# Half sums of weight blocks: added by GpSimd instead of by accumulating DMAs

## The reference, cut to what matters

```python
D_MODEL = 2048
SEQ = 256
DEPTH = 2
D_FF = 4 * D_MODEL

def sq_relu_mlp(xn, w_up, w_down):
    return jnp.square(jax.nn.relu(xn @ w_up)) @ w_down

def reference(x, ...):
    h = x
    for l in range(DEPTH):
        j = l // 2
        hn = rms_norm(h, mix_norm_g[l])
        if l % 2 == 0:
            h = h + diff_hgrn_mixer(...)
        else:
            h = h + short_conv_mixer(...)
        hn = rms_norm(h, mlp_norm_g[l])
        h = h + sq_relu_mlp(hn, mlp_w_up[l], mlp_w_down[l])
    return rms_norm(h, final_norm_g)
```

## Time and profile before

| | |
|---|---|
| median of 3 runs | 2291.91 us (2291.8 to 2291.96) |
| the profiled execution | 2291.84 us, its span 2289.8 us |
| PE busy | 2256.8 us, 99% |
| DVE busy | 1759.3 us, 77% |
| ACT busy | 1291.2 us, 56% |
| POOL busy | 289.8 us, 13% |
| granted TensorE clock, mean | 0.998 |
| bytes moved | 470.49 MB, 205 GB/s mean |
| the accumulating DMAs | 44.04 MB, 10.3% of the time of the 16 DMA engines |

### The profile page before, as it was taken

One profiled execution on the slowest core, in us unless ns is written; L12 is line 12 of the kernel. 1 busy time (PEld: TensorE's weight loads), 2 busy tenths in 40 slices (PEclk: granted clock), 3 DMA queues, 4 the chain that ended last, 5 costly groups with the idle time before them and its releaser, 6 DMA issues.

```text
span 2289.8 us, 31124 instructions
## 1 busy us (share of the span) xinstructions
PE 2256.8 (99%) x11429; PEld 1902.5 (83%) x11429; DVE 1759.3 (77%) x1882; ACT 1291.2 (56%) x1655; POOL 289.8 (13%) x409
## 2 busy tenths in 40 slices
PE   8999999999999999999999999999999999999997
PEld 7888888878788888888889999998788888888886
DVE  5778788866888888888875564657888888888885
ACT  5555555537666566566555333435665665665663
POOL 4444555510000000000000000000000000000000
PEclk9999999999999999999999999999999999999999
DMA  9555555556778678678656555556687787787754
GB/s 261 166 158 153 159 153 147 167 168 217 210 239 275 193 238 276 197 232 280 182 167 208 180 176 195 190 183 221 182 279 202 224 285 201 223 278 209 219 172 154
DMA packets 324321, 470.49 MB, mean 205 GB/s; under 512 B 13257, under 2 KB 144626, under 8 KB 318706
## 3 DMA queue, kind: packets, MB, share of 16 engines
q1 hardware_dynamic: 318114, 424.92, 56.8%
q0 software_dynamic: 6048, 44.04, 10.3%
q10 hardware_dynamic: 48, 0.02, 0.0%
HBM read 422.79 MB, written 2.10 MB: 186 GB/s over the span
## 4 chain that ended last, share of the span: by engine, by line
PE 90%; DVE 7%; ACT 1%; issue 1%; SPq 1%; DMA 0%; DVEq 0%; POOL 0%; POOLq 0%; ACTq 0%
PE pair L433 18%; PE pair L437 18%; PE pair L435 17%; PE m L1083 7%; PE m L1088 7%; PE m L1086 7%; PE pair L456 3%; PE pair L460 3%; PE pair L458 3%; DVE raw L1781 2%; DVE w_lo L524 2%; PE m L460 1%; PE m L458 1%; PE m L456 1%; PE m L934 1%
## 5 line engine op out<-in xcount | busy, mean ns | idle before, releaser
L520 ACT ACTIVATE w_hi<-raw 128x1024 fp32r<-128x1024 f32 x648 | 663.3, 1056 | 494.5 <-DVE raw L1781 242.9
L524 DVE TENSOR_TENSOR w_lo<-raw,w_hi 128x1024 fp32r<-128x1024 f32 x648 | 764.2, 1221 | 204.5 <-ACT w_hi L520 202.5
L412 DVE TENSOR_TENSOR w_lo<-raw,w_hi 128x1024 fp32r<-128x1024 f32 x320 | 400.1, 1267 | 273.5 <-ACT w_hi L401 272.2
L401 ACT ACTIVATE w_hi<-raw 128x1024 fp32r<-128x1024 f32 x320 | 337.3, 1060 | 447.1 <-PE pair L437 278.9
L433 PE MATMUL pair<-w_hi,yT_hi 128*128 128x512 f32 x1280 | 506.5, 396 | 2.5 <-DVE h L1544 0.9
L437 PE MATMUL pair<-w_hi,yT_lo 128*128 128x512 f32 x1280 | 499.1, 390 | 0.0
L435 PE MATMUL pair<-w_lo,yT_hi 128*128 128x512 f32 x1280 | 498.5, 389 | 0.0
L433 PEld LDWEIGHTS pair<-w_hi,yT_hi 128*128 128x128 f32 x1280 | 240.4, 188 | 56.1 <-issue 7.2
L437 PEld LDWEIGHTS pair<-w_hi,yT_lo 128*128 128x128 f32 x1280 | 240.3, 188 | 51.1
L435 PEld LDWEIGHTS pair<-w_lo,yT_hi 128*128 128x128 f32 x1280 | 240.7, 188 | 47.5
L433 PE MATMUL pair<-w_hi,xT_hi 128*128 128x512 f32 x640 | 255.9, 400 | 0.0
(11 more groups left out here) (168 smaller groups left out, 3104.7 us busy)
## 6 DMA issues: line engine op xcount, KB each, us to landing
raw<-in_mlp_w_up SPq DMA_DIRECT2D x128, 1024.0 KB, 7.0
raw<-in_mlp_w_down SPq DMA_DIRECT2D x256, 512.0 KB, 6.3
raw<-in_ab_w_in SPq DMA_DIRECT2D x256, 256.0 KB, 4.0
raw<-in_conv_w_in SPq DMA_DIRECT2D x48, 1024.0 KB, 5.1
raw<-raw POOLq DMA_DIRECT2D x42, 1024.0 KB, 8.7
raw<-in_ab_w_out SPq DMA_DIRECT2D x64, 256.0 KB, 4.3
raw<-in_conv_w_out SPq DMA_DIRECT2D x16, 1024.0 KB, 5.1
h<-in_x SPq DMA_DIRECT2D x4, 512.0 KB, 5.9
```

Of the source, the lines that this page charges most:

```text
L401: nc.scalar.activation(w_hi[:, ring], raw[:, slot, 2 * k:2 * k + 2], ACT.Copy).then_inc(hi_ready, 1)
L412: nc.vector.tensor_tensor(w_lo[:, ring], raw[:, slot, 2 * k:2 * k + 2], w_hi[:, ring].bitcast(F32), ALU.subtract).then_inc(lo_ready, 1)
L520: nc.scalar.activation(w_hi[:, entry % HALVES], src, ACT.Copy).then_inc(hi_ready, 1)
L524: nc.vector.tensor_tensor(w_lo[:, entry % HALVES], src, w_hi[:, entry % HALVES].bitcast(F32), ALU.subtract).then_inc(lo_ready, 1)
```

## The change

POOL adds the three half sums itself, as one instruction `tensor_tensor` over 128x2048 elements, in place, where it issued a DMA. Its semaphore rises by 1 instead of 16, and ACT's wait is counted to match. The place in POOL's queue, the waits ahead of it and every other engine's instructions and their order stay as they were: in POOL's queue 42 DMAs become 42 additions.

```diff
@@ -831,8 +831,8 @@
                         else:
                             last = {"P6": "P5", "P4": "P6"}[name]
                             pool.wait_ge(lo_ready, 2 * (slot_of(at, r, last) + 1) + 2)
-                        pool.dma_start(blocks[a][:, 1], blocks[b][:, 1], accum_op=ALU.add
-                                       ).then_inc(added[name], 16)
+                        nc.gpsimd.tensor_tensor(blocks[a][:, 1], blocks[a][:, 1], blocks[b][:, 1],
+                                                ALU.add).then_inc(added[name], 1)
 
             rstd_of(1)
             mlp(MLP0_AT, 0)
@@ -1357,7 +1357,7 @@
                         buf = buffer_of(r, BLOCK_OF[name])
                         for k in range(2):
                             if name in SUMS and (name, second) not in SUMS_DVE:
-                                eng.wait_ge(added[name], 16 * (nth(layer, r) + 1))
+                                eng.wait_ge(added[name], nth(layer, r) + 1)
                             elif name in SUMS:
                                 eng.wait_ge(sums.sem, sums.at(f"{name}{second}", nth(layer, r)))
                             else:
```

## The result

| | before | after |
|---|---|---|
| median | 2291.86 us (2291.77 to 2291.96, 4 runs) | 2443.36 us (2440.77 to 2446.9, 4 runs) |
| ratio | | 1.0662, 95% interval 1.0644 to 1.0681 |
| profiled execution, its span | 2291.84, 2289.8 us | 2446.9, 2445.0 us |
| granted clock, mean of the span | 0.998 | 0.982 |
| bytes moved | 470.49 MB | 426.45 MB |

The kernel is 151.5 us slower by the medians, 155.2 us by the spans of the two profiled executions. The prediction said 2448 us, with a range of 2430 to 2478.

What follows compares the result with a forecast made beforehand. PE was taken as the bound, with DVE close ahead: POOL sums hold DVE, costing 4.4 + 4.4 + 2.3 = 11.1 us a round, times 14 = 155, on 2291.84 gives 2447; with small waits 2448 us, range 2430 to 2478.

Steps and rivals of the forecast that it cites:

- What bounds the kernel: PE is busy 99% of the span and, where it waits for w_lo, follows on DVE's heels, so DVE's delays become PE's.
- What goes is worth nothing: The 42 accumulating DMAs are hidden; removing them gives nothing by itself, at most PE's idle 0.45 us a round.
- The length of the sum: One POOL addition of 128x2048 floats takes an estimated 4.65 us; the skill's table gives 4497 ns.
- The block B: Time DVE loses to one POOL sum: 4.65 less 0.25, so 4.4 us; lower bound 3.4.
- The place at P7: P7's sum goes in between P5's w_lo's, PE has no reserve: 4.4 us, nearly all one pause of about 4.1.
- rival (b): DVE keeps its turn; POOL enters only at holes or PSUM reads: 7.7 us a round, 2400 us in all; chance 0.08.
- The places at P6 and P4: P6's sum delays D1's second w_lo, cost 4.4 us by D2; P4's delays D3's, cost 2.3 us after 2.1 in hand.
- The clock stays up: PE's granted clock was to stay at 1.00 in the rounds, despite the new pauses.
- rival (a): The clock falls to half level behind P5's pause: 2.1 us a round, 29 us more, 2477 us; chance 0.13.
- The total: Three places cost 11.1 us a round, times 14 rounds 155 us; with small following waits, 2448 us.
- Rival (c): No exclusion: POOL's additions run beside w_lo without touching it, so no cost, 2292 us; chance 0.06.
- Rival (d): A gain of 0.45 us a round from freed DMA time, 6 us in all, 2286 us; chance 0.02.

Runs made afterwards that it cites:

- e4: Kernel after, with only P4's half sum added by POOL and those of P7 and P6 left as accumulating DMAs: 2345.03 us, ratio 1.0229.
- e1: Kernel after, with each POOL sum replaced by three fills of the same place, which write and read nothing: 2291.69 us, ratio 0.9999.
- e9: Kernel before, with the first half sums of P6 and P4 made accumulating DMAs too, five a round: 2288.3 us, ratio 0.9984.
- e6: Kernel after, with each POOL sum covering only half of the elements, the rest left out: 2349.11 us, ratio 1.0249.
- e7: Kernel after, with one tiny POOL addition ahead of P7's sum in rounds 2 to 7: 2454.2 us, one run.
- e8: Kernel after, with one tiny DVE memset ahead of P5's sums in rounds 2 to 7: 2456.51 us, one run.
- e11: Kernel after, with POOL copying the other block's half (one input) instead of adding: 2332.07 us, one run.
- e5: Kernel after, with each POOL sum cut into four instructions of 512 elements: 2405.12 us, ratio 1.0495.

## Why the prediction was right, step by step

**What bounds the kernel: right.** PE has no reserve against DVE at P5 and P7/D2, and 2.05 us at P4. e4's clean round (2.35 = 4.40 - 2.05) is that third figure measured.

**What goes is worth nothing: right.** Without the DMAs and without reads on POOL the time is the same to 0.01% (e1). Weight loads of the up projection do land in 5.9 us in the kernel after (7.0 before), and nobody was waiting for them. The bound that was given for such a gain, PE's idle time of 0.45 us in a round, isn't one: e9 made a round 0.33 us shorter and left that idle time as it was.

**The length of the sum.** Estimated at 4.65 us, it is 4.46 once POOL is in. The Trainium skill's figure that the prediction cites for it (GPSIMD Engine Reference, Elementwise — side-by-side cycle accounting, 4497 ns) was 0.04 us off, closer than the estimate from the rows. The 5.76 us of mean in the group of L834 is no measure of it: 0.99 us or more is waiting, as the prediction had warned.

**The block B = 4.4: right**, 4.3 to 4.4 in 30 of 42 cases. Estimate and correction were each off by some 0.2 (4.46 less 0.06, instead of 4.65 less 0.25), which is luck; e6's 2.21 for half the size is independent.

**The place at P7: wrong by 0.6 us in 12 rounds.** The step that failed is "a waiting POOL gets in at DVE's next boundary". One w_lo more passed, and since the next in DVE's row was L1810, which reads PSUM and isn't held, 0.64 us of POOL's 4.4 lay beside it. It cost 3.76, which is the figure of rival (b) for this place (3.8), reached by half of (b)'s mechanism. 12 x 0.64 = 7.7 us less than forecast. e7 and e8 bring this place back to 4.4. P5's pause is 3.57 and not 4.1 for the same reason.

**The places at P6 and P4: right**, 4.40 and 2.4 (8.16 to 10.55). All of B arrives by D2, and nothing catches up before the next sum except what the clock had lost.

**The clock stays up: wrong; rival (a) came true in half.** It falls behind P5's pause as (a) had said, and costs 1.6 us at D1 in seven rounds, 2.4 in five and 1.0 in the first of each layer, around (a)'s 2.1. But (a) added these to the end, and they are repaid at D2, because PE would have had to wait there for DVE in any case. What (a) didn't say is that the pause at P4, which is shorter, is enough as well: in 4 of 14 rounds of the profiled execution, for 1.5 us each, 6 us in all. How often it happens differs from one execution to the next, and probably makes the 6 us between the fastest and the slowest of the four runs (clocks 0.989 and 0.982); this isn't shown, as only one of the four has a profile.

**The total.** 12 x 10.55 + 2 x 11.15 = 149 from the blocks, where the prediction's 14 x 11.1 had 155, and 6 from the clock. So the 155.2 measured equal the 155 forecast by two errors of 6 us with opposite signs. The mechanism is shown (e1, e6, e11), the prices of the places too (e4, e7, the table); that the number agrees to 0.2 us in the profiled execution is chance. By the medians the kernel lost 151.5 us, and the 2448 said is 4.6 us too high.

**Rival (c)**, no exclusion, is refuted by 42 w_lo's of 4.98 to 5.63 us. **Rival (d)**, a gain by freed DMA time, by e1.

## What to carry to other kernels

Before work goes to an idle GpSimd, ask which of VectorE's instructions will lie beside it: against those with two inputs in SBUF a GpSimd instruction that reads SBUF wasn't parallel in any run here, it was inserted, at GpSimd's speed. Here the same sum costs VectorE 4.40 us on GpSimd, 2.29 us on VectorE itself and nothing as an accumulating DMA, and so the DMA, slowest of the three by itself (8.7 us), is the right place here, where the DMA engines have room. Costs measured for single places don't add up when a pause also lowers TensorE's clock (such a loss was repaid where the next wait for VectorE stood, and stayed where none did), nor when a sum gets its turn at another point than it does beside the others.

## What the runs showed of the hardware that was not expected

- TensorE's clock fell behind a pause of 2.09 us in 13 rounds of 14 and stayed up behind one just as long in the other (e4, both rows above). Each fall cost 1.5 to 1.6 us at that place. A longer pause wasn't certain to bring it down: behind one of 3.26 us it stayed up in two rounds of 14 (e5). Behind the pauses of up to 1.7 us it never fell (e6: 0.998 over the span).
- A GpSimd instruction that waits for VectorE got in at the first boundary, one instruction later, or only when VectorE ran out of work, almost always the same for one place of one kernel and differently for the same place of another (5.45, 6.54 and 8.78 us with the wait in). Tiny instructions on either engine shift it (e7, e8).
- Memsets of 128x2048 floats by GpSimd, 1.81 us each, ran beside VectorE's two-input subtractions without changing them by more than 10 ns (longest 1228 ns, median 1219).
